# One-layer Hymba/Conformer/S5 trunk with hierarchical MoE: expert jobs overlapped with their neighbours, down weights in 8 KB rows, setup loads moved forward

## What is computed

```python
mod = silu(c) @ w_ada + b_ada            # 6 vectors: shift1, scale1, gate1, shift2, scale2, gate2
h = rms_norm(x, norm1_g) * (1 + scale1) + shift1
p = h @ w_in                             # 4096 columns: conv value, conv gate, ssm input, ssm gate
y_conv = silu(layer_norm(causal_depthwise_conv31(value * sigmoid(gate))))
y_ssm  = gelu(s5_scan(u) + d * u) * sigmoid(ssm_gate)        # 64 groups of 16 channels, 64 complex states
x = x + gate1 * (concat(rms_norm(y_conv), rms_norm(y_ssm)) @ w_out)
h = rms_norm(x, norm2_g) * (1 + scale2) + shift2
# router: best of 4 groups, then the best 2 of its 8 experts, weights comb
y = sum over 32 experts of comb[:, e] * (silu(h @ w_gate[e]) * (h @ w_up[e])) @ w_down[e]   # 2048 -> 512 -> 2048
x = x + gate2 * y
return rms_norm(x, final_norm_g)
```

## Time and profile before

| | us |
|---|---|
| median of 3 runs | 1630.73 (1630.63 to 1631.09) |
| the profiled execution, own time | 1632.0 |
| its span in the trace | 1630.2 |
| PE busy | 1463.2 (90%) |
| DVE busy | 518.3 (32%) |
| ACT busy | 222.0 (14%) |
| HBM read | 562.62 MB, 346 GB/s over the span |

### The profile page before, as it was taken

One profiled execution on the slowest core, in us unless ns is written; L12 is line 12 of the kernel. 1 busy time (PEld: TensorE's weight loads), 2 busy tenths in 40 slices (PEclk: granted clock), 3 DMA queues, 4 the chain that ended last, 5 costly groups with the idle time before them and its releaser, 6 DMA issues.

```text
span 1630.2 us, 17467 instructions
## 1 busy us (share of the span) xinstructions
PE 1463.2 (90%) x6620; PEld 733.7 (45%) x6620; DVE 518.3 (32%) x936; ACT 222.0 (14%) x397; POOL 88.1 (5%) x112
## 2 busy tenths in 40 slices
PE   1999999999985979899989989989989989989986
PEld 0546667776632444335335325325335335335432
DVE  0636978599921231021121021012012012112103
ACT  1222100014200121011002002002002002002001
POOL 0000021030100026000000000000000000000000
PEclk9999999999997989999999999999999999999998
DMA  8999789986374437999999999999999999999994
GB/s 302 408 416 404 270 332 390 385 325 253 110 266 128 146 112 300 404 402 372 410 398 384 414 394 387 416 391 380 419 387 419 395 388 416 395 391 415 385 395 172
DMA packets 160124, 565.36 MB, mean 347 GB/s; under 512 B 23274, under 2 KB 23410, under 8 KB 114066
## 3 DMA queue, kind: packets, MB, share of 16 engines
q1 hardware_dynamic: 144896, 559.98, 87.6%
q10 hardware_dynamic: 15186, 4.81, 1.3%
HBM read 562.62 MB, written 2.13 MB: 346 GB/s over the span
## 4 chain that ended last, share of the span: by engine, by line
PE 64%; DMA 7%; issue 6%; PEld 5%; DVE 5%; ACTq 5%; SPq 4%; ACT 3%; PEldq 1%; DVEq 0%
PE ps L860 25%; PE ps L560 10%; PE ps L864 9%; PE ps L818 7%; DMA ring<-in_exp_w_down 7%; PE ps L799 7%; SPq L499 4%; PE ps L530 4%; PEld ps L560 2%; ACTq L1050 2%; ACTq L906 2%; PEld ps L721 1%; PE ps L523 1%; PEldq L725 1%; DVE arena L1418 1%
## 5 line engine op out<-in xcount | busy, mean ns | idle before, releaser
L860 PE MATMUL ps<-ring,arena 128*64 128x512 f32 x2048 | 454.0, 595 | 9.2 <-issue 9.2
L860 PEld LDWEIGHTS ps<-ring,arena 128*64 128x64 f32 x2048 | 157.1, 137 | 279.0 <-issue 275.4
L864 PE MATMUL ps<-ring,arena 128*64 128x512 f32 x1024 | 233.8, 597 | 46.8 <-DMA ring<-in_exp_w_down 40.0
L560 PE MATMUL ps<-arena,ring 128*128 128x256 f32 x1024 | 230.2, 383 | 6.6 <-ACT arena L978 3.3
L560 PEld LDWEIGHTS ps<-arena,ring 128*128 128x128 f32 x1024 | 193.8, 191 | 50.0 <-issue 24.3
L864 PEld LDWEIGHTS ps<-ring,arena 128*64 128x64 f32 x1024 | 77.1, 136 | 196.4 <-issue 167.1
L799 PE MATMUL ps<-arena 128*128 128x256 f32 x512 | 132.3, 411 | 8.2 <-ACT arena L1098 5.3
L799 PEld LDWEIGHTS ps<-arena 128*128 128x128 f32 x512 | 120.4, 305 | 30.7 <-issue 14.7
L721 PE MATMUL ps<-ring,arena 128*128 128x512 f32 x256 | 114.4, 605 | 20.8 <-DVE arena L1508 20.7
L530 PE MATMUL ps<-ring,ccol 128*32 128x512 f32 x768 | 94.5, 612 | 37.5 <-ACT ccol L916 36.0
L1633 DVE TENSOR_TENSOR arena<-arena,ps 128x512 f32<-128x512 f32 x16 | 11.0, 688 | 348.8 <-PEq L874 348.8
(11 more groups left out here) (262 smaller groups left out, 701.5 us busy)
## 6 DMA issues: line engine op xcount, KB each, us to landing
ring<-in_exp_w_gate SPq DMA_DIRECT2D x128, 1024.0 KB, 10.6
ring<-in_exp_w_up SPq DMA_DIRECT2D x128, 1024.0 KB, 13.2
ring<-in_exp_w_down SPq DMA_DIRECT2D x128, 1024.0 KB, 14.3
ring<-in_w_ada SPq DMA_DIRECT2D x96, 1024.0 KB, 10.6
ring<-in_w_in SPq DMA_DIRECT2D x32, 1024.0 KB, 9.0
ring<-in_w_out SPq DMA_DIRECT2D x16, 1024.0 KB, 10.9
arena<-in_x SPq DMA_DIRECT2D x2, 1024.0 KB, 8.0
arena<-in_x SPq DMA_DIRECT2D x1, 2048.0 KB, 10.6
```

The costliest lines, as they stand in the source:

```text
L560: last = mm(ps[:, j // 2, (j % 2) * T:(j % 2 + 1) * T], ring[:, s, kk * N + j * P:kk * N + (j + 1) * P], hT[:, k, :], start=(k == 0 and j ...
L860: last = mm(ps[half, stage, :], xT[:, k, slot:slot + SLOTS], ring[:, s, kk * N:(kk + 1) * N], start=(k == 0), stop=(k == KD - 1), skip_gro ...
L864: last = mm(ps[half, 2 + pr, :], hidT[pr][:, kk, half], ring[:, s, kk * N:(kk + 1) * N], start=(kk == 0), stop=(kk == 3), skip_group_check ...
```

## The change

1. **Down weights.** A unit is now 128 whole rows of `w_down`, 8 KB each. A step of two units holds one 128-row slice of the inner dimension for two experts; it adds to all four column quarters, in four PSUM banks (2 to 5). Only the last of a pair's four steps ends the sums.
2. **Jobs overlapped.** PE's loop body is: down steps of job j, each followed by one eighth of the gather of job j+1; then 16 gate and up steps of job j+1, the first eight each followed by one eighth of the combine of job j. The first job's gather, gate and up stand ahead of the loop; the last job's down and combine (`combine_last`, one product at a time, so that each pair's part is added by itself) behind it. ACT's squares of `acc` are made once, at the end, and the final norm is cut by token tile.
3. **Residual copy.** ACT copies x1 into `x1p`, laid out so that the gather's stationary operand is contiguous. `acc` is x1 itself.
4. **Drives.** No `apart`: each of the eight products takes 32 rows of `uT` and `driveT`.
5. **Loads.** silu(c) is computed after three loads; `conv_w` is loaded in 16 and 15 rows; the C loads come after the squares of x. Router weights are loaded there too, in 16 partitions with rows of 2 and 4 KB, turned by PE in 36 transposes (k = 13) and copied by DVE. ACT moves them into place after the tables and issues the two bias loads there.

The core of the diff:

```diff
 JOB_ORDER = ...
-    [(2, pr, u, x) for u in range(4) for pr in range(2) for x in range(2)]
+    [(2, pr, u, x) for pr in range(2) for u in range(4) for x in range(2)]
...
-        acc = at(32, 16 * KB).rearrange("p (t d) -> p t d", t=TT)
+        x1p = at(32, 16 * KB).rearrange("p (t k q) -> p t k q", t=TT, k=KD)
+        acc = x1
...
-                        src = w_down[bass.ds(e, 1), :, :, u * N:(u + 1) * N].rearrange("e p j n -> (e p) j n")
-                        dst = ring[:, s, :].rearrange("p (j n) -> p j n", j=4)
+                        src = w_down[bass.ds(e, 1), u * P:(u + 1) * P, :].rearrange("e p n -> (e p) n")
...
+                if k == 13:
+                    pe.wait_ge(wr_landed, 16 * 5)
+                    for e in range(NG + EXP):
...
+                        last = tr(dst, wst[:, o:o + (P - 1) * width + 1:width], KD)
+                    last.then_inc(wr_turned, 1)
...
-                                last = mm(ps[:, 4 + r, c * T:(c + 1) * T], driveT[:, c, q, :], apart[:, r, :],
+                                rr = slice(32 * r, 32 * r + 32)
+                                last = mm(ps[:, 4 + r, c * T:(c + 1) * T], driveT[rr, c, q, :], uT[rr, q, :],
                                           start=True, stop=True)
...
+            def down(j, pr, u):
+                if u == 0:
+                    pe.wait_ge(hidden_stored, j * 2 + pr + 1)
+                m = 32 + 8 * pr + 2 * u
+                weights(j, m)
+                for n in range(4):
+                    if u == 0 and pr == 1:
+                        pe.wait_ge(down_stored, j * 8 + n + 1)
+                    for x in range(2):
+                        half = slice(64 * x, 64 * x + 64)
+                        last = mm(ps[half, 2 + n, :], hidT[pr][:, u, half],
+                                  ring[:, (m + x) % RING, n * N:(n + 1) * N], start=(u == 0), stop=(u == 3),
+                                  skip_group_check=True)
...
+                    if u == 3:
+                        pe.drain().then_inc(down_done, 1)
...
             def job(j):
+                for i in range(8):
+                    down(j, i // 4, i % 4)
+                    if i == 0:
+                        turn_hidden(j, 1)
                         pe.wait_ge(scatter_ready, j + 1)
+                    gather(j + 1, i)
+                for i in range(16):
+                    gate_up(j + 1, i)
+                    if i < 8:
+                        combine(j, i)
+                    if i == 8:
+                        turn_hidden(j + 1, 0)
+                    if i == 9:
+                        pe.wait_ge(added, j * 8 + 8)
+                        turn_picks(j + 1)
...
-                if g + 1 in DRIVE_AT:
...
-                        nc.scalar.copy(apart[rr, r, :], uT[rr, q, :]).then_inc(apart_ready, 1)
...
+            act.wait_ge(wr_staged, 1)
+            nc.scalar.copy(wr, wr_early).then_inc(wr_ready, 1)
...
             def job(j, next_picks):
+                for i in range(8):
+                    if i % 4 == 3:
+                        store_down(j, i // 4)
+                    even_tokens(j + 1, i)
+                for m in range(8):
+                    add(j, m, m // 2, m % 2, 6 + m % 2)
+                dve.wait_ge(added, j * 8 + 8)
+                hidden(j + 1, 0)
+                store_picks(j + 1)
+                next_picks()
+                hidden(j + 1, 1)
```

More of the change, by code:

```diff
@@ L877, in _, with gather @@
-            with pe.Fori(0, NB) as j:
+            def gather(j, i):
+                if i == 0:
+                    pe.wait_ge(picks_ready, j + 1)
+                for k in (2 * i, 2 * i + 1):
+                    if k >= 2:
+                        pe.wait_ge((tok_even, tok_odd)[k % 2], j * 8 + k // 2)
+                    for t in range(TT):
+                        last = mm(ps[:, 6 + k % 2, 0:T], x1p[:, t, k, :], pick[:, t, :], start=(t == 0), stop=(t == 1))
+                    last.then_inc(gathered, 1)
@@ new lines, in combine @@
+            def combine(j, m):
+                n, t = divmod(m, 2)
+                if m == 0:
+                    pe.wait_ge(down_stored, j * 8 + 8)
+                    pe.wait_ge(scatter_ready, j + 1)
+                    pe.wait_ge(tok_even, j * 8 + 16)
+                    pe.wait_ge(tok_odd, j * 8 + 16)
+                if m >= 2:
+                    pe.wait_ge(added, j * 8 + m - 1)
+                for pr in range(2):
+                    last = mm(ps[:, 6 + t, :], wpickT[:, pr, t * P:(t + 1) * P], yexp[pr][:, n, :],
+                              start=(pr == 0), stop=(pr == 1))
+                last.then_inc(combined, 1)
@@ L886, in _ @@
+            for m in range(8, 16):
+                combine_last(j_last, m)
         @block.scalar
@@ L1661, in first_listed @@
+            hidden(0, 0)
+            store_picks(0)
+            counted_picks(1)
+            hidden(0, 1)
+            with dve.Fori(0, NB - 2) as j:
+                job(j, lambda: counted_picks(j + 2))
             def first_listed():
```

409 lines of the change are left out of this document (226 added, 183 removed).

## The result

The changed kernel takes 1590.36 us (median of 4 runs, 1590.18 to 1591.41), the kernel before 1630.91 us on the same chip (4 runs): ratio 0.9751 [0.9734, 0.9768], 40.6 us less. I had forecast 1549.0 (1526 to 1578), so the sign was right, and half of the gain was missing. The profiled execution has a span of 1589.5 us.

What follows compares the result with a forecast made beforehand. PE was taken as starting late, then nearly always busy except a DVE-bound convolution and waits for router loads and down weights. Terms 5.0 + 8.6 + 23.4 + 43.0 + 2.0 = 82.0 off 1632.0 gave 1550.0, median 1549 us (1526 to 1578).

Steps and rivals of the forecast that it cites:

- Start, -5.0: Up to the first chunk and its store: earlier silu(c) and a split conv_w load save 7 us, less 2.0 for ACT.
- the other reading: ACT's queue at the start: conv_w's issue queued behind the two C loads; sum at most 5 us worse.
- Drives, -8.6: Ahead of the convolution's second half: four drives each 2.6 us shorter, less 1.8 us waiting for DVE.
- Rival 2: Drives: row groups run one after another, so the drives give nothing; 1558 us, chance 0.13.
- Router loads, -23.4: Between last read and router: PE's 20.67 us wait goes, and 2.75 us of low clock behind it.
- Expert jobs, -43.0: Expert jobs: from 1014.2 to 971.2 us through fewer waits and a contiguous operand, less the cost of more tiling changes.
- A contiguous stationary operand, 17.2 us less: Gather in the expert jobs: 256 products fall from 132.3 us to 115.1, as chunk products of the same size take.
- A change costs about 0.12 us: Expert jobs: 142 more changes between products of 64 and 128 columns cost 17.0 us more.
- rival 1: Expert jobs: each change of column grouping drains the array, 38 us more; 1587 us, chance 0.12.
- The term for the waits, 40.0: Expert jobs: PE's 40.0 us of waits for down weights go, as the ring fills during down steps.
- Rival 3: Expert jobs: a down unit still takes 2.71 us, about 10 us of waits return; 1559 us, chance 0.08.
- End, -2: After the last product: two of DVE's four half rows lie beside the last square; 2.4 less 0.4 us.

Runs made afterwards that it cites:

- p1: The kernel before with its conv load alone split into 16 and 15 rows, the C loads still ahead of it: 1630.4 us, ratio 0.9990.
- s4: The changed kernel with the conv weights loaded in one transfer of 31 rows again: 1595.7 us, ratio 0.9781 to the kernel before.
- s1: The changed kernel with ScalarE's Sqrt first, then router loads, copies, and the C loads last with their own semaphore: 1578.0 us, ratio 0.9672.
- s2: The changed kernel with the five router-weight loads issued behind the Sqrt and the eight copies, C loads left in place: 1595.4 us, ratio 0.9783.
- d1: The kernel before with the drive products alone changed, over 32 rows straight from u, without the copies: 1625.6 us, ratio 0.9952.
- g1: The changed kernel with the copy of x1 left unpermuted, so gather steps load every 16th column: 1600.3 us, ratio 0.9804.
- m1: The changed kernel with one of each pair of gather steps moved into the down step's middle, 98 more tiling changes: 1606.8 us, ratio 0.9844.
- x1: The changed kernel without TensorE's wait, value load, second loop and branch at the job loop's exit: 1580.6 us, ratio 0.9684.
- w1: The changed kernel with each down unit loaded in rows of 2 KB again instead of 8 KB: 1596.1 us, ratio 0.9779.
- x2: The changed kernel with TensorE's load of the last job's number moved into the first job, both loops and branch kept: 1589.6 us, ratio 0.9744.
- x3: The changed kernel with that number loaded in the first job and one TensorE loop running to it, no branch: 1580.9 us, ratio 0.9687.
- s3: The changed kernel with the Sqrt ahead of the router loads and the C loads on SyncE's queue behind the eighth weight unit: 1580.2 us, ratio 0.9686.
- c2: The changed kernel with x3's single loop, and the C loads behind the parameters' Sin with their own semaphore: 1569.6 us, ratio 0.9612.
- c3: c2 with the norm2 gain and last four parts of b_ada issued behind the C loads, with their own semaphore: 1569.0 us, ratio 0.9615.

## Why the prediction was right or wrong, step by step

*Start, -5.0: the step that failed, 22.6 us of the 41.* Measured +17.6. The step was "which issue stalls next?". I took the reading by the cited rule on 31 rows, called the issue of the C loads the other reading, and gave that reading "at most the 5 us of this term worse". p1 with s4 shows that the other reading was the true one for the kernel before, and s1 and s2 that the issues at the C loads are what holds ScalarE after it. Its price was wrong too: I let ScalarE "stall there by up to some 10 us, when PE can still work on units landed". Measured, the two C loads and the router loads behind them hold the queue for 34 us, and TensorE cannot go past its fifth unit without the Sqrt behind them. The row had the numbers: c_im and conv_w were shown with 0.69 and 24.06 us, so 2048 + 31 rows had to find room before anything else, in the same stretch of time and beside the same stream. I should have asked what drains ahead of a stalled issue, and at what pace.

Three smaller terms of this sum came out otherwise too. The router transposes, which I had among units that TensorE must wait for, stand in a stretch without such waits (49.29 to 79.1 us) and take 4.1 us of it, at half the clock. The idle time ahead of the first chunk, which I had as saved, is still there, 2.88 us for 2.87. And for ScalarE's added work ahead of the gate product I charged 2.0 us; the wait there rose from 3.27 to 3.85.

*The pace.* The profile counts the packets of each queue. For the 18.12 us of c_im's issue in the changed kernel (15.29 to 33.41 us; packets, MB, share of 16 engines; q1 is the queue of the weight units, q10 ScalarE's):

```profile
q1 hardware_dynamic: 1016, 7.39, 98.7%
q10 hardware_dynamic: 1016, 0.07, 4.2%
```

One small row goes for one large one; in the 10.63 us of the group weights' issue it is 580 to 580. The 1016 small ones have 69 bytes each on the mean. So nearly all of them were not rows of the C loads, which have 256 bytes, but of the four gain and bias loads issued by 8.8 us, 1024 rows of 64 bytes. What drained while c_im's issue stalled was other small rows, which I had not counted at all. Whether moving those alone, with the C loads left in place, would have freed the start was not run. The Trainium skill's page "DMA: Bandwidth & Descriptors", section Queues, rings and completion order, has each engine take turns between the queues by the packet. The trace agrees with it, with the numbers above. I had read that page for another rule.

*The rule that I did use.* One DMA engine for 31 rows: no row shows the engine, and the 24 us are not its work (p1). What s4 shows is 5.3 us for the form with 31 rows, with the first weight units 4 us apart. This is what one overloaded engine would do, so the rule may hold; my use of it did not.

*Drives, -8.6.* Measured -7.0. A drive costs 1.15 us, so 2.57 less each where I took 2.6; the wait of the fourth drive for DVE, 1.30, was in the sum (1.8). The mechanism holds (d1: 8.0 up to the convolution; here 5.3, with the 2.65 us of low clock against it). Rival 2 is refuted.

*Router loads, -23.4.* Measured -22.7: the 20.7 us of idle time and the low clock behind it are gone. The last pair of permuted copies delays a copy on ScalarE, and TensorE waits 1.03 us for it at 580.48; I had it at up to 1.

*Expert jobs, -43.0.* Measured -25.9. Three terms account for the difference and a little more. "A contiguous stationary operand, 17.2 us less" was worth 9.9 (g1), 7.3 short: I had compared page groups of which the chunk products share neither the waits nor the neighbours of the gather's. "A change costs about 0.12 us": 0.17 (m1), so 142 changes cost 24 us and not 17, 7 more; the 0.39 of rival 1 is refuted. (The 0.12 does not come out of the two times beside it: 3.65 less 3.49 is 0.16, and with half a change to each side of the step that is the price of one.) And the sum had no term at all for the way out of the loop, 9.8 us (x1): in the kernel before that code stood behind TensorE's last product, where it cost nothing. I looked at which products moved, and not at which loads and branches now stand between products. Together 24 us for the 17.1 missing. (The Trainium skill's page "TensorEngine Tiling (Array Packing)", section Key Properties, has a change of tiling mode drain TensorE: it is right that a change costs, and m1 puts the price at under half of an explicit drain here.) Of the 7 us that went the other way 1.4 are in the waits left over (1.1 us, I had 2.5). The rest is about what the idle time called issue lost, which the sum left as it was: 9.2 us ahead of gate and up products, 6.5 ahead of combine products, 5.4 ahead of down products and 2.0 ahead of transposes in the kernel before, 23.1 in all; 23.4 in the changed one, of which 7.3 are the way out of the loop, so 16.1. No run isolates it. The term for the waits, 40.0, was right in size, and w1 tells how it divides: about 34 by the order, about 6 by the rows. Rival 3's mechanism is refuted: the units come at 423 GB/s. That the measured 1590.4 lies near rival 1's 1587 is chance.

*End, -2.* Measured -2.7.

## What to carry to other kernels

A stalled DMA issue names the place, not the culprit: count the rows issued ahead of it on that queue, and expect them to drain at one for each large row of the stream beside them (1016 to 1016 here); then no time-critical work may stand behind such loads on the issuing engine, nor may their landing be counted on a semaphore that something early waits for. When work is software-pipelined across a loop's end, the loop's exit comes between products: count the loads of values and the branches there, and prefer one loop with a bound read early to two loops with a branch between them. And do not take the granted clock of a busy stretch over from one trace: with the same start, the kernel before had 1.00 from 60 to 65 us and d1 0.50, and its gate product came 7.4 us later.

## What the runs showed of the hardware that I had not expected

- A branch over a loop's code, with that code, cost TensorE about 6 us; the load of a value from memory with its wait 1.0 us, and nothing visible when it stands among products (x2, x3).
- A load of 31 rows behind nothing issues in 0.57 us and still delays the weight stream: units about 4 us apart instead of 2.5 (s4).
- Loads of 1024 rows issue in 0.39 or 18.12 us according to what is still queued (s1 and the changed kernel).
- In four versions of the start (s1, s3, c2, c3) with different waits the first chunk comes at 70.4 to 71.2 us. Small rows drain beside the stream wherever they are put, the granted clock lies between 0.5 and 0.8 from 50 to 70 us (0.50 in c2, 0.67 in s3, 0.51 and 0.81 in c3), and the 36 router transposes take 4.18 us in each. Which of the three sets the 70 us is open; none of the four held the clock up through that stretch.
